# Root and reciprocal of fourteen norms as one power of -0.5 on GpSimd

## What is computed

```python
def rms_norm(x, g):
    xf = x.astype(jnp.float32)
    y = xf * lax.rsqrt(jnp.mean(xf * xf, axis=-1, keepdims=True) + EPS)
    return (y * g.astype(jnp.float32)).astype(x.dtype)
def layer_norm(x, g, b):
    ...
    y = (xf - mu) * lax.rsqrt(var + EPS)
```

## Time and profile before

| | us |
|---|---|
| median of three runs | 1731.7 (1731.04 to 1733.73) |
| the profiled execution | 1730.45 |
| its span, first to last instruction | 1728.7 |

### The profile page before, as it was taken

One profiled execution on the slowest core, in us unless ns is written; L12 is line 12 of the kernel. 1 busy time (PEld: TensorE's weight loads), 2 busy tenths in 40 slices (PEclk: granted clock), 3 DMA queues, 4 the chain that ended last, 5 costly groups with the idle time before them and its releaser, 6 DMA issues.

```text
span 1728.7 us, 22955 instructions
## 1 busy us (share of the span) xinstructions
PE 1635.8 (95%) x8269; PEld 1399.4 (81%) x8269; DVE 1437.0 (83%) x2698; ACT 781.7 (45%) x1310; POOL 580.5 (34%) x414
## 2 busy tenths in 40 slices
PE   7999988989999999999998999998999999999998
PEld 5876555667899999999998999997877777777787
DVE  2577887875886799999998999937989989999897
ACT  3232122331244434448998999953333333333332
POOL 0000000000001244444555555523554545545560
PEclk9998999999999999999999999999999999999999
DMA  6111412224436799998999999999999999999995
GB/s 205 56 42 33 45 49 86 71 87 173 134 108 203 265 329 338 329 326 289 375 384 347 414 388 387 373 362 378 404 403 404 400 403 400 404 403 402 400 389 176
DMA packets 155351, 482.37 MB, mean 279 GB/s; under 512 B 26031, under 2 KB 43119, under 8 KB 153063
## 3 DMA queue, kind: packets, MB, share of 16 engines
q1 hardware_dynamic: 99943, 279.57, 45.4%
q0 software_dynamic: 55296, 201.35, 30.7%
HBM read 426.17 MB, written 54.42 MB: 278 GB/s over the span
## 4 chain that ended last, share of the span: by engine, by line
PE 62%; DVE 18%; DMA 12%; ACT 4%; issue 3%; SPq 0%; POOL 0%; DVEq 0%; ACTq 0%; POOLq 0%
PE ps L808 21%; PE ps L953 16%; DMA raw<-in_v 9%; PE ps L563 6%; PE ps L762 5%; PE ps L579 4%; PE ps L929 4%; DVE lo L1529 3%; DMA gelu_matrix<-gest 3%; ACT hi L1072 2%; DVE ring L1690 2%; DVE acc L1694 2%; DVE caccb L1398 1%; PE ps L591 1%; DVE gA L1789 1%
## 5 line engine op out<-in xcount | busy, mean ns | idle before, releaser
L1072 ACT ACTIVATE hi<-raw 128x1024 fp32r<-128x1024 f32 x256 | 270.6, 1057 | 347.9 <-PE ps L953 187.8
L1311 POOL DMA_INDIRECT ring<-in_u,idx x192 | 285.1, 1485 | 422.4 <-DVE hu L1690 259.6
L1529 DVE TENSOR_TENSOR lo<-raw,hi 128x1024 fp32r<-128x1024 f32 x256 | 313.2, 1223 | 135.0 <-ACT hi L1072 133.0
L1311 POOL DMA_INDIRECT ring<-in_v,idx x192 | 282.8, 1473 | 285.9 <-DVE acc L1694 272.4
L808 PE MATMUL ps<-xh,hi 128*128 128x384 f32 x1024 | 351.3, 343 | 10.7 <-DVE lo L1529 10.0
L808 PE MATMUL ps<-xh,lo 128*128 128x384 f32 x1024 | 344.2, 336 | 0.0
L808 PE MATMUL ps<-xl,hi 128*128 128x384 f32 x1024 | 344.1, 336 | 0.0
L953 PE MATMUL ps<-hi,ah 128*128 128x512 f32 x768 | 240.7, 395 | 19.1 <-DVE al L1822 11.7
L1694 DVE SCALAR_TENSOR_TENSOR acc<-ring,hu,acc 128x1024 f32<-128x1024 f32 x192 | 245.5, 1278 | 0.1
L953 PE MATMUL ps<-lo,ah 128*128 128x512 f32 x768 | 237.8, 391 | 0.0
L953 PE MATMUL ps<-hi,al 128*128 128x512 f32 x768 | 237.1, 390 | 0.0
(11 more groups left out here) (219 smaller groups left out, 1957.2 us busy)
## 6 DMA issues: line engine op xcount, KB each, us to landing
raw<-in_uT SPq DMA_DIRECT2D x128, 512.0 KB, 7.3
raw<-in_v SPq DMA_DIRECT2D x128, 512.0 KB, 8.9
wring<-in_wblk SPq DMA_DIRECT2D x58, 512.0 KB, 3.5
gelu_matrix<-gest SPq DMA_DIRECT2D x64, 384.0 KB, 9.2
gate_matrix<-Gs SPq DMA_DIRECT2D x16, 1536.0 KB, 8.4
gel<-gelu_matrix SPq DMA_DIRECT2D x64, 384.0 KB, 8.5
Gl<-gate_matrix SPq DMA_DIRECT2D x64, 384.0 KB, 10.9
wring<-in_wblk SPq DMA_DIRECT2D x16, 256.0 KB, 2.6
```

The lines of the kernel that those rows point to most:

```text
L1072: nc.scalar.activation(hi[:, s % 2, :], raw[:, s % RAWS, :], ACT.Copy).then_inc(s_hi, 1)
L1311: pool.indirect_dma_start(ring[:, r % SLOTS, :], None, table, bass.IndirectOffsetOnAxis(idx[:, t, c:c + 1], 0)).then_inc(g_in[r % SLOTS], 16)
L1529: nc.vector.tensor_tensor(lo[:, s % 2, :], raw[:, s % RAWS, :], hi[:, s % 2, :].bitcast(F32), ALU.subtract).then_inc(s_lo, 1)
```

## The change

ScalarE no longer takes the root: the activation is an Identity with the same bias, so `rs` or `rsb` receives the mean square plus epsilon. GpSimd has a new helper `rstd`, which waits for ScalarE's count, raises the tile to the power of -0.5 in place (a two-input instruction with a constant column, broadcast, as the exponent) and counts `F[bank]`. Its calls are put among the chunk sums. VectorE's `rstd` only waits for `F[bank]`.

```diff
@@ scalar
-                nc.scalar.activation(dst, p, ACT.Sqrt, bias=epst[:, :]).then_inc(s_rt, 1)
+                nc.scalar.activation(dst, p, ACT.Identity, bias=epst[:, :]).then_inc(s_rt, 1)
@@ gpsimd
-                                               (epst[:, :], EPS))):
+                                               (epst[:, :], EPS), (mhalf[:, :], -0.5))):
...
+            def rstd(name, dst):
+
+                nrt[0] += 1
+                pool.wait_ge(s_rt, nrt[0])
+                nc.gpsimd.tensor_tensor(dst, dst, mhalf.broadcast_to([P, dst.shape[1]]), ALU.pow).then_inc(
+                    F[use[name][0]], 1)
+
+            for name in ("ms1", "Kn", "Q0n", "Q1n", "Q2n", "Q3n"):
+                rstd(name, rs[:, 0, :])
+            rstd("msA", rs[:, 0, 0:DT])
+            rstd("var", rs[:, 1, 0:DT])
+            rstd("msC", rs[:, 1, 0:DT])
+            rstd("ms2", rs[:, 0, 0:DT])
             chunk_sum(rsb[:, 0, :], lambda k: caccb[:, (k - 1) % CC, :], CC, s_conv_b)
             chunk_sum(mgb[:, CC, :], lambda k: mgb[:, CC + k, :], CC, s_sqc, CC)
+            rstd("varb", rsb[:, 1, :])
             chunk_sum(mgb[:, 0, :], lambda k: mgb[:, k, :], CC, s_sqa, CC)
+            rstd("msAb", rsb[:, 0, :])
             chunk_sum(mgb[:, CC, :], lambda k: mgb[:, CC + k, :], CC, s_sqcr, CC)
+            rstd("msCb", rsb[:, 1, :])
             chunk_sum(xn[:, 0, DT:T], lambda k: xn[:, k, DT:T], DC, s_sqh, DC)
+            rstd("ms2b", rsb[:, 0, :])
@@ vector
             def rstd(name, dst):
-                nrt[0] += 1
-                dve.wait_ge(s_rt, nrt[0])
                 bank, n = use[name]
-                nc.vector.reciprocal(dst, dst).then_inc(F[bank], 1)
                 dve.wait_ge(F[bank], n)
```

More of the change, by code:

```diff
@@ L232, in hymba_peer @@
         epst = sb("epst", [P, 1])
+        mhalf = sb("mhalf", [P, 1])
         ijg = sb("ijg", [P, len(TILES), 3, NPICK])
@@ L341, in hymba_peer @@
         s_sq1 = sem("sq1_ready")
-        s_rt = sem("root_ready")
+        s_rt = sem("mean_square_copied")
         s_rs = sem("rstd_ready")
@@ L1295, in chunk_sum @@
                 add.then_inc(s_sum, 1)
+            nrt = [0]
+            def rstd(name, dst):
[9 more added lines that the diff above has]
+            rstd("ms2", rs[:, 0, 0:DT])
             chunk_sum(rsb[:, 0, :], lambda k: caccb[:, (k - 1) % CC, :], CC, s_conv_b)
             chunk_sum(mgb[:, CC, :], lambda k: mgb[:, CC + k, :], CC, s_sqc, CC)
+            rstd("varb", rsb[:, 1, :])
             chunk_sum(mgb[:, 0, :], lambda k: mgb[:, k, :], CC, s_sqa, CC)
+            rstd("msAb", rsb[:, 0, :])
             chunk_sum(mgb[:, CC, :], lambda k: mgb[:, CC + k, :], CC, s_sqcr, CC)
+            rstd("msCb", rsb[:, 1, :])
             chunk_sum(xn[:, 0, DT:T], lambda k: xn[:, k, DT:T], DC, s_sqh, DC)
+            rstd("ms2b", rsb[:, 0, :])
             pool.wait_ge(s_o2, 16 * 15)
@@ L1326, in ready @@
                 return region(name)
-            nrt = [0]
             def rstd(name, dst):
-                nrt[0] += 1
-                dve.wait_ge(s_rt, nrt[0])
                 bank, n = use[name]
-                nc.vector.reciprocal(dst, dst).then_inc(F[bank], 1)
                 dve.wait_ge(F[bank], n)
```

## The result

The changed kernel takes 2588.63 us (median of four runs, 2585.77 to 2588.94), the kernel before 1731.65 us (four runs, 1731.04 to 1733.73). The ratio is 1.494, with an interval of 1.492 to 1.497. The forecast was 1789 us with a range up to 1945. It said slower, and the kernel is slower, but by 857 us and not by 58. One execution of the kernel before, beside the first experiments, took 4204.57 us at a granted clock of 1.00; nothing here explains it, and no ratio uses it.

A forecast was written before the change was run, and what follows sets the result against it. TensorE work mostly bounds the chain; norms matter where TensorE idles or late VectorE spends the time. Terms 8.1 + 31.5 + 12.4 + 1.3 + 6.3 − 1.4 − 0.3 = +57.9 on 1730.45 gave 1789 us, range 1720 to 1945.

The forecast's parts named there:

- x: Length of one power on GpSimd: taken as 13 us at 576 columns, 8.7 at 384, 4.35 at 192.
- rival (e): Powers on GpSimd slower still, 30/20/10 us: about 1947 us; everything above rival (d) had chance 0.23.
- The single file at Kn to Q3n: Five norms before the attention scores share one tile, so their powers run one after another: +31.5 us, the largest term.
- var: Norm whose power queues on GpSimd behind another norm's, so its result is used later: +12.4 us.
- msC: Norm costing x − 2.39, less 5.0 us in which VectorE waits for TensorE's next results: +1.3 us.
- msCb: Late norm: power done in time, gain capped by TensorE reaching that operand about 0.3 us earlier: −0.3 us.
- ms2b: Norm whose result only the late queries use, with only rankings behind it on VectorE: 0 us.
- (a): Power costs little more than an add on GpSimd: −7.2 us, 1723 us, or about 1719; chance 0.17.
- (b): Power costs about what the reciprocal does, 4 to 5 us at 576 columns: 1730 us, no change; chance 0.10.
- (c): Power at one function's price, 8.1/5.4/2.7 us: +17.3, 1748 us; the forecast between it and (d) had chance 0.50.
- (d): Power at two functions' price, 18/12/6 us: 1832 us; the forecast between (c) and it had chance 0.50.
- (f): Table loads on ScalarE don't vanish, the next function's load replacing them; only one norm would notice, +1.3 us; no chance given.

The follow-up runs named there:

- the run of ten products: Changed kernel with ten chained GpSimd products in place of each power, 12.2, 9.0 and 5.8 us long by width: 1794.42 us, ratio 1.035.
- the run of the late norms: Kernel before with the power only at the four 192-column norms of group B, the other ten keeping root and reciprocal: 1830.2 us.
- the product: Changed kernel with one GpSimd product in place of each power, all waits and hand-overs kept: 1719.88 us, ratio 0.993.
- the early table: Kernel before with ScalarE's reciprocal root for root and reciprocal, plus a one-column activation loading its table before the first norm's wait: 1717.39 us, ratio 0.991.

## Why the prediction missed

**The step that failed is the size of x.** The prediction said: "If a function costs 4.6 adds on GpSimd too, one is 8.1 us at 576 and two with the product 18 us. I take the middle". It carried a ratio of two instructions on VectorE over to another engine, on which no row showed any function at all. Measured is 92.19 us, 80 products of the same shape (92.19/1.145), and 7.1 times the value taken. The cap of 30 us had nothing behind it either; the text itself says that no row caps the price, and then the range stopped there, at 1945, 2 us under the 1947 that rival (e) gives for it. A range with an upper end that comes from no row ought to have been worked out from the sensitivity, which stood there and was right: about ten us of time for one of power. Measured: (858.5 − 57.9)/(92.19 − 13) = 10.1.

**The single file at Kn to Q3n** was forecast and is there, but with a wrong link. The prediction let ScalarE wait for VectorE's product, because the five norms share the tile rs. In the trace that product ends 1.5 us before ScalarE starts; what ScalarE waits for is TensorE's mean, which waits for the bank pair that the power frees. With the mean at full clock, 1.13 us, this way round would be about x + 2.1, and that the prediction had x + 2.14 out of other terms is luck. In the run of ten products, where the last mean takes 1.21 us, the powers start 14.39 us apart, x + 2.2. In the changed kernel the period is 95.45 us, x + 3.26, since the mean runs at half clock after the long idling: four times 1.13 us, 4.5 of the 5.2 that are missing there. Most of the rest is the first projection at the lower clock, 18.64 us in place of 17.69. No run takes away the tile's or the bank's wait. But GpSimd does its powers one after another in any case, so 92.19 of each 95.45 us would remain.

**ms1, var, ms2, varb, msAb** hold to 0.4, 2.4, 0.2, 0.0 and 0.0 us with the measured x. The 0.0 of msAb rests on a slack of "some 2 us", so it is partly luck. The 2.4 us at var are made before var, behind the 84.32 us of idling: from the first scores to the second it is 12.02 us in place of 9.48, with the first eight score matmuls at 2.08 us in place of 1.16 and a granted clock of 0.50 to 0.55 from 604 to 610 us. The hand-overs (0.09 and 0.12 us) are a little below the 0.15 taken. The vanished load at ms1 and the two powers back to back at var are as forecast; msA's and var's powers are one row of two:

```profile
741.14 122.99 POOL L1304 TENSOR_TENSOR rs<-rs,mhalf 128x384 f32<-128x384 f32 x2 [137.57 <-ACT rs L980]
```

**msC** was mis-sized by a constant. I took off 5.0 us because VectorE waits that long for TensorE behind it. The run of ten products and the changed kernel both lie 4.6 us above the formula, so only 0.4 us of that is slack at these two values of x. VectorE's waits there are no reserve: the matmuls that it waits for wait for VectorE's `hT` of the step before, as in this row of the changed kernel:

```profile
952.77 13.14 PE L580 MATMUL ps<-mg,wring 128*128 128x384 f32 x32 [56.73 <-DVE hT L1523]
```

**msCb** lies 2.2 us above its 24.5, and 2.0 in the run of the late norms. It is the lower clock again: after 22.82 us of idling the mean takes 0.98 us in place of 0.49, and after another 22.19 us of idling the 56 matmuls of the row below take 11.30 us (granted clock 0.50 from 1216 to 1220 us), where 64 of them took 10.93 before, or 9.6 us for 56:

```profile
1216.83 11.30 PE L580 MATMUL ps<-mgb,wring 128*128 128x192 f32 x56 [22.19 <-DVE mgb L1518]
```

So the lower clock behind the new idle times costs about 10 of the 39.6 us: 5.2 at Kn to Q3n, 2.4 counted at var, 2.2 at msCb. The prediction left it out of its sum with "up to +4".

**ms2b** was put at nothing with the words "VectorE has only rankings behind it, which TensorE's dense loop doesn't wait for at once". The dense loop doesn't, but the queries ahead of it do, through ScalarE's copies. At 5.8 us the step holds (81.37 us as before), at 30.9 it costs 22.7. So the cover is some 8 us thick (30.9 − 22.7, an estimate from these two points), and I had named a cover without its thickness.

**What stays open.** The dense part is 1.8 us longer; between profiled executions whose dense parts hold the same work, that part differs by 2 to 4 us (1231.3 before, 1233.1 after, 1235.6 with the reciprocal root), so this isn't explained. Why the instruction takes 160 ns a column isn't shown, only that the exponent and half of the partitions don't matter. Powers on other engines were not tried, nor a power on GpSimd in another form, with the exponent as a constant of the instruction.

**The rivals.** (a) is what the product shows: with x = 1.15 the change as ordered gains 0.7%. (b), (c) and (d) are points of a curve that the ten products confirm at one place, to 8 us. (e) has the right side and, at 30 us, a third of the measured x. (f) is excluded by the trace at ms1 and by the count of table loads, 23 after and 29 before.

## What to carry to other kernels

An operation that no row of the profile shows has no price until it has been run once by itself; until then the range must follow the path's sensitivity to it, and no ratio from another engine may close it. Before a function moves to an idle engine, ask first whether the engine that does it now can do it in one instruction: here the reciprocal root from ScalarE's table takes the place of root and reciprocal, and the two versions with it gain 1%. For each cover that lets an edit count as nothing, write down how thick it is, and don't count as slack a wait for something that itself waits for you. Where an edit makes an engine idle, look at the clock of the matmuls behind the pause. And when a resource is freed by a slower instruction than before, here the bank pair by the power, ask who waits for it.

## What the runs showed of the hardware

- GpSimd's two-input power in float32 costs 160 ns a column: 92.19, 61.51 and 30.92 us at 576, 384 and 192 columns, the same for exponents −0.5 and −1 and for 64 or 128 partitions. The product of the same form takes 1.145, 0.826 and 0.507 us.
- A logarithm and an exponential on ScalarE, one behind the other, loaded a table of 1.28 us each, every time.
- The reciprocal root from ScalarE's table takes as long as the root: 0.74 us at 576 columns.
- TensorE's clock at ms1 by what stood before: after 14.16 us of idling (ten products) the projection starts at the lower level, 1.2 GHz, and so it does after 6.98 us (the kernel before). After 3.15 and 3.20 us (the product, the reciprocal root) it starts at the higher level and the granted clock falls to 0.50 between 18 and 22 us, while it runs. After 1.86 us (the early table) it stays at 1.00. Each is one traced execution.
- A shorter idle time need not shorten the slow stretch. Without the root TensorE idled 1.28 us less, and the projection ran 1.00 us longer, in one traced execution of each kernel.
- Short matmuls in a serial chain run at the lower level too: the mean of four took 2.26 us in place of 1.13 behind each idle time of 82 to 85 us.
